# Two-layer S5 and attention trunk on one core: the rotation tables moved to other steps of the order, and block 3's powers held behind a gate

## The reference

```python
for l in range(2):
    x = x + 0.5 * swiglu(rms_norm(x, g[0]), w_in[l, 0], w_out[l, 0])     # D_FF = 2816
    h = rms_norm(x, g[1])
    if l == 0:  x = x + s5_mixer(h, ...)       # diagonal complex state space, 64 groups x 64 states
    else:       x = x + mla_attention(h, ...)
    x = x + 0.5 * swiglu(rms_norm(x, g[2]), w_in[l, 1], w_out[l, 1])
    ...
def swiglu(h, w_in, w_out):
    gu = h @ w_in
    return (silu(gu[..., :D_FF]) * gu[..., D_FF:]) @ w_out
```

## Time and profile before

| What | Value |
|---|---|
| median of 3 runs (lowest to highest) | 1794.61 us (1794.11 to 1796.55) |
| the profiled execution: its time, its span | 1793.16 us, 1791.4 us |
| PE busy | 1765.9 us, 99% of the span |
| DVE, ACT, POOL busy | 927.9, 655.5, 323.7 us |
| mean granted TensorE clock | 0.997 |
| OUT of the first part begins | 136.49 us |

### The profile page before, as it was taken

The page is one execution under the profiler, slowest core; times in us unless marked ns, Lnnn a source line. Parts: engine busy times, 40 slices in busy tenths (PEclk is TensorE's granted clock), DMA queues, the critical chain, the costliest instruction groups (busy, mean ns, idle before and its releaser), DMA issues.

```text
span 1791.4 us, 21523 instructions
## 1 busy us (share of the span) xinstructions
PE 1765.9 (99%) x8142; PEld 1451.5 (81%) x8142; DVE 927.9 (52%) x1065; ACT 655.5 (37%) x901; POOL 323.7 (18%) x277
## 2 busy tenths in 40 slices
PE   9999899999999999999999999999999999999998
PEld 6887788879888888888888888888777888888887
DVE  7768978647555344433374334333674544444333
ACT  6332233347434333332253333322474433333222
POOL 8997533016014000000000000000200200000000
PEclk9999999999999999999999999999999999999999
DMA  5363635588432222222223222222210332222221
GB/s 199 119 171 118 184 133 161 157 312 305 130 102 97 95 94 94 102 97 94 94 83 107 103 95 94 94 101 99 96 46 1 108 105 102 96 94 94 99 90 48
DMA packets 80785, 206.46 MB, mean 115 GB/s; under 512 B 24048, under 2 KB 34416, under 8 KB 79696
## 3 DMA queue, kind: packets, MB, share of 16 engines
q1 hardware_dynamic: 69664, 189.86, 31.7%
q0 software_dynamic: 2592, 13.51, 2.2%
q10 hardware_dynamic: 8464, 2.20, 0.5%
HBM read 182.46 MB, written 23.07 MB: 115 GB/s over the span
## 4 chain that ended last, share of the span: by engine, by line
PE 89%; DVE 4%; POOL 3%; issue 2%; ACT 2%; DMA 1%; SPq 0%; ACTq 0%; DVEq 0%; POOLq 0%
PE bank L1622 28%; PE bank L1624 27%; PE bank L1623 27%; DVE w_split L1173 1%; PE bank L1954 1%; PE bank L1800 1%; PE bank L1817 1%; PE bank L1810 1%; ACT w_split L756 1%; PE bank L1933 1%; DVE ops_out L1222 0%; PE bank L1652 0%; DVE up L1217 0%; DMA x_res<-xT 0%; DVE ops_out L1219 0%
## 5 line engine op out<-in xcount | busy, mean ns | idle before, releaser
L1173 DVE TENSOR_TENSOR w_split<-w_raw,w_split 128x1024 fp32r<-128x1024 f32 x296 | 401.0, 1359 | 623.1 <-ACT w_split L756 622.5
L1622 PE MATMUL bank<-h_split,w_split 128*128 128x512 f32 x1504 | 588.9, 392 | 3.6 <-DVE w_split L1319 1.6
L1624 PE MATMUL bank<-h_split,w_split 128*128 128x512 f32 x1504 | 585.3, 389 | 0.0
L1623 PE MATMUL bank<-h_split,w_split 128*128 128x512 f32 x1504 | 585.2, 389 | 0.0
L756 ACT ACTIVATE w_split<-w_raw 128x1024 fp32r<-128x1024 f32 x296 | 312.1, 1058 | 637.8 <-PE bank L1624 630.1
L1622 PE MATMUL bank<-g_split,w_split 128*128 128x512 f32 (+1 forms) x854 | 330.3, 387 | 8.1 <-DVE w_split L1173 4.9
L1622 PEld LDWEIGHTS bank<-h_split,w_split 128*128 128x128 f32 x1504 | 282.3, 188 | 66.4 <-issue 2.3
L1623 PEld LDWEIGHTS bank<-h_split,w_split 128*128 128x128 f32 x1504 | 282.4, 188 | 59.3 <-issue 1.2
L1624 PEld LDWEIGHTS bank<-h_split,w_split 128*128 128x128 f32 x1504 | 282.3, 188 | 58.6
L1624 PE MATMUL bank<-g_split,w_split 128*128 128x512 f32 (+1 forms) x854 | 329.3, 386 | 0.0
L1623 PE MATMUL bank<-g_split,w_split 128*128 128x512 f32 (+1 forms) x854 | 329.2, 385 | 0.0
(11 more groups left out here) (297 smaller groups left out, 1187.2 us busy)
## 6 DMA issues: line engine op xcount, KB each, us to landing
w_raw<-wstream SPq DMA_DIRECT2D x296, 512.0 KB, 3.4
op_slot<-s_ops SPq DMA_DIRECT2D x5, 2048.0 KB, 10.6
s_ops<-ops_out SPq DMA_DIRECT2D x16, 512.0 KB, 3.0
op_slot<-s_ops POOLq DMA_DIRECT2D x3, 2048.0 KB, 14.0
s_ops<-c_pow POOLq DMA_DIRECT2D x8, 512.0 KB, 4.8
s_ops<-k_window SPq DMA_DIRECT2D x64, 64.0 KB, 3.4
x_res<-xT SPq DMA_DIRECT2D x8, 256.0 KB, 6.5
s_u<-x_gained ACTq DMA_DIRECT2D x8, 256.0 KB, 6.2
```

What stands on the lines that cost most here:

```text
L1173: tt(W[:, r, 1, :], RAW[:, r, :], W[:, r, 0, :].bitcast(F32), ALU.subtract).then_inc(s_lo, 1)
L1622: mm(bank, hi, x_hi, start=start, stop=True, skip_group_check=True)
L1623: mm(bank, hi, x_lo, start=False, stop=True, skip_group_check=True)
L1624: return mm(bank, lo, x_hi, start=False, stop=True, skip_group_check=True)
```

## The change

`TABLES_AT` gets other places. Block 0's tables go from OUT d = 0 of the first part to d = 2, block 1's from d = 1 to d = 5, block 2's from d = 4 to IN tile 0 of the second part; those of blocks 3, 4 and 6 stay at IN tiles 1, 4 and 8; block 5's go from IN tile 6 to 7 and block 7's from IN tile 10 to 9. As the loop over IN begins at tile 1, a call for tile 0 is added in DVE's `ffn_in`. SP's stores of the tables move with them. POOL waits for `s_g_lo` at HALF, the low part of the eleventh and last gate of the first part, before `make_powers(3)`.

```diff
--- before.py
+++ after.py
@@ -84,8 +84,8 @@
            (FFN0A2, IN, 2): 5, (FFN0A2, IN, 5): 6, (FFN0A2, IN, 8): 7}
 TAPS_AT = {(FFN0A1, IN, 5): 0, (FFN0A1, IN, 8): 1, (FFN0A1, IN, 10): 2, (FFN0A1, OUT, 3): 3, (FFN0A1, OUT, 6): 4,
            (FFN0A2, IN, 3): 5, (FFN0A2, IN, 6): 6, (FFN0A2, IN, 9): 7}
-TABLES_AT = {(FFN0A1, OUT, 0): 0, (FFN0A1, OUT, 1): 1, (FFN0A1, OUT, 4): 2, (FFN0A2, IN, 1): 3, (FFN0A2, IN, 4): 4,
-             (FFN0A2, IN, 6): 5, (FFN0A2, IN, 8): 6, (FFN0A2, IN, 10): 7}
+TABLES_AT = {(FFN0A1, OUT, 2): 0, (FFN0A1, OUT, 5): 1, (FFN0A2, IN, 0): 2, (FFN0A2, IN, 1): 3, (FFN0A2, IN, 4): 4,
+             (FFN0A2, IN, 7): 5, (FFN0A2, IN, 8): 6, (FFN0A2, IN, 9): 7}
 
 N_IN0A, N_S5, N_IN0B, N_KV, N_LAT, N_DQ, N_IN1B, N_FINAL = range(8)
 
@@ -645,6 +645,7 @@
             powers(tt, link, PA, 7, t1, t2)
             nc.gpsimd.memset(TM[:, 0:8], 0.0).then_inc(s_near, 1)
             pool.wait_ge(s_near, 1)
+            pool.wait_ge(s_g_lo, HALF)
             for k in range(3, BLOCKS):
                 make_powers(k)
 
@@ -1265,6 +1266,8 @@
                     dve.wait_ge(s_rstd, n + 1)
                 gated(stage, 0, 0, stage + 2)
                 split(stage, 3)
+                if stage == FFN0A2:
+                    s5_ops(stage, IN, 0)
                 ffn_in_loop(stage)
 
             def add_ffn(stage, d):
```

## The result

| What | Before | After |
|---|---|---|
| median (lowest to highest), 11 runs each | 1793.1 us (1790.81 to 1796.55) | 1798.31 us (1791.83 to 1802.19) |
| ratio after/before, 95% interval | | 1.0025 (1.0016 to 1.0033) |
| the profiled execution: its time, its span | 1793.16, 1791.4 us | 1802.19, 1800.4 us |
| mean granted clock | 0.997 | 0.996 |
| OUT of the first part begins | 136.49 us | 139.43 us |

The change costs time: 4.5 us by the ratio (2.9 to 5.9), where +9.3 was forecast. The sign and the range held, the size was twice too large.

What follows compares the result with a forecast made beforehand. PE bounds the kernel, busy 1765.9 of 1791.4 us, so a change on POOL and DVE acts only where PE waits. Gains and losses at ten places sum to +9.3, a median of 1803.9 us, range 1789 to 1811.

Steps and rivals of the forecast that it cites:

- Steps 1 to 3: First part's OUT: last gate's wait goes, -4.9; block 3's powers late, +0.2; wait from block 1's tables goes, -7.8 us.
- Step 4: First part's OUT: block 0's tables at d = 2 held beside POOL's block 4, next split late, +7.7 us.
- Step 5: Start of second part: block 3's taps stored late, PE waits for ACT's copies, +5.9 us.
- Step 2: First part's OUT: block 3's powers start later and are ready just before their turn, +0.2 us.
- Rival A: Block 0's tables fit POOL's pause, so late split and late taps vanish: 1790.3 us, chance 0.15.
- Step 6: End of first part's OUT: block 1's tables at d = 5 fall in POOL's pause, nothing.
- Step 7: Second part, IN: block 2's tables at tile 0 delay the read of tile 2, +1.2 us.
- Step 8: Second part, IN: block 4's unmoved tables carry DVE's delay on, wait for L1185 grows, +5.5 us.
- Step 9: Second part, IN: block 5's tables go from tile 6 to 7, nothing.
- Step 10: Second part, start of OUT: block 7's tables ahead of tile 10's gate make it late, +1.5 us, no clock loss.
- Rival B: Second part keeps its margins, with no cost from block 2's, 4's and 7's tables: 1795.7 us, chance 0.11.
- Rival D: The gating fails: DVE's gate is late for another reason and the first wait stays, 1808.8 us, chance 0.06.

Runs made afterwards that it cites:

- experiment 5: The changed kernel, but block 4's six operations on POOL work on one group of eight: 1786.35 us, ratio 0.996 to before.
- experiment 6: The changed kernel with the tables of blocks 0 to 7 at OUT 5, IN 0, 1, 3, 6, 7, 8, 10: 1791.27 us, ratio 0.9983 to before.
- experiment 7: The changed kernel with the tables of blocks 0 to 7 at OUT 5, 6, IN 0, 3, 6, 7, 8, 10: 1788.07 us, ratio 0.9964 to before.
- experiment 8: The changed kernel with the tables of blocks 0 to 7 at OUT 6, IN 0, 3, 5, 6, 7, 9, 10: 1784.86 us, ratio 0.9949 to before.
- experiment 3: The changed kernel with block 7's tables, and its taps with them, back at IN tile 10: 1795.76 us, ratio 1.0009 to before.
- experiment 4: The changed kernel with block 0's tables at OUT d = 3 for d = 2, behind block 3's taps: 1794.53 us, ratio 0.9999 to before.
- experiment 2: The changed kernel without POOL's wait for the last gate, only the tables' new places: 1791.36 us, ratio 0.9996 to before.
- experiment 1: The kernel of before with only POOL's wait for the last gate added, tables at their old places: 1796.58 us, ratio 1.0024 to before.

## Why the prediction was wrong in its size

The sections make the account. The kernels 5 to 8 have no long wait in the first, and it takes 63.91 us. What a wait costs with its start-up and clock is taken from the starts in PE's timeline, by how much they lie further apart than 0.227 us.

- **Steps 1 to 3** (-4.9, +0.2, -7.8, together -12.5). Right. Before's first section is 76.13, and 76.13 - 63.91 = 12.2. Step 2 alone was low: PE waits 0.77 us for block 3's powers in after and in all kernels with the gate (0.75 to 0.78), for 0.2 in all.
- **Step 4** (+7.7, idle 5 and clock 2.7). Right in place and cause, by experiment 5. Measured: 6.1 for the wait of 4.28 and 1.0 for that of 0.73, 7.1; in experiment 3's execution 4.9. Of the six table operations only L1222 (189.94, 0.69 us) was free.
- **Step 5** (+5.9). Right in place and cause; measured 8.5 (6.4 up to the first matmul, 2.1 behind it); in experiment 3's execution 10.0. SP took 7.53 us to issue the eight window stores, for 6.08 in the earlier trace rows. Steps 4 and 5 together: 15.6 for 13.6, and 14.8 in experiment 3: they trade, as the prediction said. How the sum falls between them hangs on one hold more or less. Rival A, which lets both vanish, is out: the last table operation was done at 193.3, not before the turn at 186.86 (188.65 and 184.37 in experiment 3).
- **Step 6** (0). Right: block 1's tables ran free, and no later wait goes back to them.
- **Step 7** (+1.2, the read of tile 2). After has hardly such a wait: PE's matmul at 264.59 starts as soon as the read of tile 2 is done, 0.3 us late, 0.4 with the next ones. Timelines of after, DVE and PE:

```profile
263.85 0.69 DVE L1186 TENSOR_TENSOR gate<-gate,bank 128x512 f32<-128x512 f32 x1 [0.70 <-ACT gate L763]
```

```profile
264.05 0.39 PE L1627 MATMUL bank<-h_split,w_split 128*128 128x512 f32 x1
...
264.59 0.50 PE L1625 MATMUL bank<-h_split,w_split 128*128 128x512 f32 x1
```

Experiments 5, 4 and 2 have the places of after in this part and no wait of 6 us at its start, and there PE idles for this read 1.14, 2.21 and 2.87 us (1.4, 4.1 and 4.7 with start-up and clock). So for a DVE without a lead the bounds of 0 to 2 held in one and were too low in two, and the failure is that steps 5 and 7 were added though the one feeds on the other: while PE waited 6.27 us at the start of the part, DVE ran ahead. Against the turn of block 5 the fourth product stands at 252.67 - 251.87 = 0.80 in after, and at 235.58 - 233.81 = 1.77 in experiment 5, 1.0 later, which is the difference of 1.4 and 0.4.
- **Step 8** (+5.5). This is the step that failed: that block 4's tables "carry DVE's delay on", idle 4.3 us and 2 of clock. The wait is 0.82 us, and it is 0.75 in experiment 5, where DVE had no lead; experiments 2 and 4 have no idle time marked there. The delay isn't carried at all. Timelines of after, DVE and then PE (the row of x16 is the turn of block 6):

```profile
252.67 1.15 DVE L1220 TENSOR_TENSOR ops_out<-u_pow 128x512 f32<-128x512 f32 x1
...
267.41 4.42 DVE L1174 TENSOR_TENSOR w_split<-w_raw,w_split 128x1024 fp32r<-128x1024 f32 x2
...
271.75 0.68 DVE L1184 TENSOR_TENSOR gate<-bank,rstd 128x512 f32<-128x512 f32 x1
...
284.95 1.12 DVE L1217 TENSOR_TENSOR gate<-u_pow 128x512 f32<-128x512 f32 x1
```

```profile
251.87 0.63 PE L1698 MATMUL bank<-c_pow,b_pow 128*16 128x128 f32 x16
...
286.57 0.63 PE L1698 MATMUL bank<-c_pow,b_pow 128*16 128x128 f32 x16
```

and of before, DVE and then PE:

```profile
257.92 6.97 DVE L1173 TENSOR_TENSOR w_split<-w_raw,w_split 128x1024 fp32r<-128x1024 f32 x2
...
264.81 0.68 DVE L1183 TENSOR_TENSOR gate<-bank,rstd 128x512 f32<-128x512 f32 x1
...
278.02 1.12 DVE L1216 TENSOR_TENSOR gate<-u_pow 128x512 f32<-128x512 f32 x1
```

```profile
279.60 0.63 PE L1695 MATMUL bank<-c_pow,b_pow 128*16 128x128 f32 x16
```

The first table operation starts 1.6 us ahead of the turn in both (284.95 and 286.57; 278.02 and 279.60), and in experiment 5 as well. DVE's delay is gone by the gate of tile 3. Counted back from the turn of block 6, the read of tile 2 starts 22.7 us ahead in after (263.85) and in experiment 5 (246.77), for 24.75 before (254.85): 2.0 late. The gate of tile 3 starts 14.82 ahead in after (271.75) and 14.86 in experiment 5 (254.65), for 14.79 before (264.81): on time. Between the two stand the splits, 4.42 us in after and 4.41 in experiment 5 for 6.97 before. A hold ends with POOL's block: in after the last arithmetic of block 6's powers was done when they asked (its store issue is at 267.24), while in before they asked at 257.92, just behind the start of L587 (257.52). I had priced a late DVE by the holds ahead of it and left out that, being late, it meets the end of POOL's block and is held less. With steps 7 and 8 at nothing the forecast's sum is +2.6, and with steps 4 and 5 at their measured size +4.6.
- **Step 9** (0). Right: no wait at tiles 7 to 9.
- **Step 10** (+1.5). Right in place: 1.66 us at 353.89, the clock stays at 1.00. Measured 61.80 - 59.84 = 1.96, with the start-up; experiment 3 takes 1.95 back.

The measured terms add up. First section: -12.2 for steps 1 to 3, +7.1 for step 4, +6.4 for the idle time of step 5, and 0.2 that I can't place, +1.5. Second: +2.1 behind step 5's wait, +0.4 for the read of tile 2 and 0.1 unplaced, +2.6. Third: +2.0. Rival B (the second part keeps its margins) was right for steps 7 and 8 and wrong for step 10. Rival D is out.

On this place of the Trainium skill: the row of 185.73 above shows a product of two SBUF inputs held 4.17 us, from 0.6 us after POOL's store issue (185.13) to 1.0 us behind the end of L574. The Trainium skill, "SBUF — State Buffer", "Who interferes with whom", infers that descriptor writing doesn't hold a tensor_tensor of this kind. The row disagrees in that the hold begins 0.9 us ahead of L574 (186.65); that the store's issue alone would do it is not shown, and a row of experiment 8, in the last section, is against it. For step 4 going by the trace was right: the operation asked there was held.

## What to carry to other kernels

When two engines take turns, ask for each moved operation which instructions of the other it will meet at its new time, and lay both engines out in one table: here the tables moved alone cost nothing that the ratio shows, the gate alone some 4 us by other waits, and the two waits of the change stand in neither. Don't add up waits along a path: a wait of the bound engine gives the others a lead, and an operation that comes late can meet the end of what would have held it, so each later wait has to be worked out from the state that the earlier ones leave. And compare sections of the trace between fixed points, since a start that varies by 5 us between executions hides a change of this size.

## What was not expected of the hardware

A DVE operation asked 0.6 us into POOL's store issue, with more instructions of POOL behind it, is held through the issues and through the POOL instruction after them. In after it is L1220 (185.73, 4.17 us; L589 at 185.13), in experiment 5 L1220 there (173.54, 4.15 us; its issue at 172.91), and in the traces of experiments 1, 2, 6 and 7 one of 4.17 to 4.19 us each. Experiment 5 is the clearest, as POOL's arithmetic before it is small: the product held 4.15 us has only the issues and L575 beside it. But one asked 0.2 to 0.3 us after the issue began went through (also the splits at 213.24 in before and 254.71 in experiment 6, 1.22 us each), in DVE's and POOL's timelines of before:

```profile
181.60 0.68 DVE L1222 TENSOR_TENSOR ops_out<-ops_out,up 128x512 f32<-128x512 f32 x1
```

```profile
181.42 0.95 POOL L589 DMA_DIRECT2D s_ops<-c_pow  x1 [0.30 <-POOL b_pow L587]
```

Two rows bound this, from DVE's timelines of experiments 8 and 4, one fence each:

```profile
285.55 1.11 DVE L1219 TENSOR_TENSOR ops_out<-u_pow 128x512 f32<-128x512 f32 x1
```

```profile
182.54 1.11 DVE L1217 TENSOR_TENSOR gate<-u_pow 128x512 f32<-128x512 f32 x1
```

The first was asked 0.60 us into the issue of block 7's store (284.95), behind which POOL has nothing before 346.43, and it went free: so the hold needs the instructions behind the store's issue. Which of them, the load's issue or L574, wasn't tried. The second began 0.1 us into block 4's issue (182.46); it and the three products behind it went free, and POOL's L574 took 4.93 us for some 2.3 (in experiment 8, at 206.12, 4.91). So a block of POOL has such a hold in store unless DVE is already in its row of operations when the issue begins. The hold is longer than the usual turn beside POOL's arithmetic (2.5 to 3.5). Longer still is the start of a block whose L574 and L579 follow each other at once: in after a split asked at 146.23, 0.3 us ahead of block 3's L574 (146.57 to 148.84), took 5.93 us, past the end of L579 (151.06), so that DVE wasn't let in between the two; in experiment 3 the same (143.74, 5.93 us).
